# A hybrid decoder step on one Trainium2 core: the final rows with buffers of their own, and their residual sum on GpSimd

## What is computed

```python
    h = rmsnorm(x, norm2_g[l]) * (1 + sc2) + sh2
    x = x + g2 * moe(h, router_w, router_b, moe_w_gate[l], moe_w_up[l], moe_w_down[l])
y = rmsnorm(x, final_norm_g)
```

## Time and profile before

| | us |
|---|---|
| median of three runs | 1424.47 |
| the profiled execution, its own time | 1426.68 |
| its span in the profile | 1425.1 |
| busy in the span: PE, DVE, ACT, POOL | 1141.1, 699.1, 579.0, 127.0 |
| first gather of the final rows issued | 1362.7 |
| last normalisation ends | 1422.9 |
| POOL idle in the final stage because of stores | 25.8 |

### The profile page before, as it was taken

The page is one execution under the profiler, slowest core; times in us unless marked ns, Lnnn a source line. Parts: engine busy times, 40 slices in busy tenths (PEclk is TensorE's granted clock), DMA queues, the critical chain, the costliest instruction groups (busy, mean ns, idle before and its releaser), DMA issues.

```text
span 1425.1 us, 18556 instructions
## 1 busy us (share of the span) xinstructions
PE 1141.1 (80%) x6899; PEld 639.2 (45%) x6900; DVE 699.1 (49%) x1029; ACT 579.0 (41%) x850; POOL 127.0 (9%) x135
## 2 busy tenths in 40 slices
PE   3799579549898989898779995029899999999810
PEld 0355256436566666665444453014445544444400
DVE  2434334344435454544733335428765686656557
ACT  2222324133535353535531113027755566555433
POOL 0000001000000000000010000522111111111032
PEclk9899789759999999999798998559999999999955
DMA  9763200062313232383142440068977797779255
GB/s 344 282 227 142 54 0 0 9 167 55 100 49 90 60 90 60 90 295 103 47 121 68 140 163 31 0 236 321 381 267 261 290 373 276 284 257 368 103 189 182
DMA packets 122341, 234.43 MB, mean 164 GB/s; under 512 B 11079, under 2 KB 54569, under 8 KB 119200
## 3 DMA queue, kind: packets, MB, share of 16 engines
q1 hardware_dynamic: 111760, 200.37, 41.3%
q0 software_dynamic: 7200, 21.06, 4.0%
q10 hardware_dynamic: 3312, 12.06, 2.1%
HBM read 197.60 MB, written 35.64 MB: 164 GB/s over the span
## 4 chain that ended last, share of the span: by engine, by line
PE 63%; DVE 13%; DMA 10%; ACT 5%; issue 5%; POOL 2%; SPq 1%; DVEq 0%; POOLq 0%; ACTq 0%
PE banks L1576 7%; PE banks L1577 6%; PE banks L1578 6%; PE banks L1915 5%; PE banks L1917 5%; PE banks L1916 5%; PE banks L1737 3%; DMA arena<-in_moe_w_gate_dram 3%; PE banks L1751 2%; PE banks L1765 2%; DVE arena L1237 2%; PE banks L1934 2%; PE banks L1936 2%; PE banks L1935 2%; PE banks L1856 2%
## 5 line engine op out<-in xcount | busy, mean ns | idle before, releaser
L1469 DVE SCALAR_TENSOR_TENSOR arena<-arena 128x2048 f16<-128x2048 f32 x96 | 217.5, 2287 | 80.8 <-ACT arena L959 80.7
L959 ACT ACTIVATE arena<-arena 128x2048 f16<-128x2048 f32 x96 | 180.5, 1907 | 92.7 <-DMA arena<-in_moe_w_up_dram 53.8
L1576 PE MATMUL banks<-arena 128*128 128x384 f16 (+5 forms) x576 | 191.5, 332 | 16.1 <-DVE arena L1119 12.4
L1577 PE MATMUL banks<-arena 128*128 128x384 f16 (+5 forms) x576 | 190.9, 331 | 0.0
L1578 PE MATMUL banks<-arena 128*128 128x384 f16 (+5 forms) x576 | 190.7, 331 | 0.0
L1915 PE MATMUL banks<-arena 128*128 128x512 f16 x368 | 141.0, 383 | 9.8 <-DVE arena L1482 9.8
L1917 PE MATMUL banks<-arena 128*128 128x512 f16 x368 | 140.7, 382 | 0.0
L1916 PE MATMUL banks<-arena 128*128 128x512 f16 x368 | 140.6, 382 | 0.0
L854 ACT ACTIVATE arena<-banks 128x512 f32<-128x512 f32 (+3 forms) x96 | 49.3, 514 | 129.9 <-PE banks L1751 129.9
L1237 DVE CUSTOM_DVE_ANT_0 arena<-banks,arena 128x128 f32<-128x128 f32 (+7 forms) x96 | 72.3, 753 | 46.0 <-PE banks L1737 45.8
L846 ACT ACTIVATE arena<-arena 128x128 f32<-128x128 f32 (+7 forms) x96 | 74.3, 774 | 28.3 <-DVE arena L1240 27.2
(11 more groups left out here) (325 smaller groups left out, 1694.1 us busy)
## 6 DMA issues: line engine op xcount, KB each, us to landing
arena<-in_moe_w_gate_dram SPq DMA_DIRECT2D x32, 1024.0 KB, 8.6
arena<-in_moe_w_up_dram SPq DMA_DIRECT2D x32, 1024.0 KB, 8.3
arena<-in_moe_w_down_dram SPq DMA_DIRECT2D x32, 1024.0 KB, 6.5
arena<-in_w_ada_dram SPq DMA_DIRECT2D x24, 1024.0 KB, 7.5
slot_rows<-arena ACTq DMA_DIRECT2D x23, 512.0 KB, 6.8
out_dram<-arena SPq DMA_DIRECT2D x20, 512.0 KB, 2.6
arena<-in_w_in_dram SPq DMA_DIRECT2D x18, 512.0 KB, 7.0
arena<-in_x_prompt_dram SPq DMA_DIRECT2D x16, 512.0 KB, 8.6
```

Source lines behind the costliest of these rows:

```text
L959: A(w_hi[s][p // 2][:, (p % 2) * PIECE:(p % 2 + 1) * PIECE], stage[g % RING], ACT.Copy, scale=WS).then_inc(phi_ok, 1)
L1469: v.scalar_tensor_tensor(out=w_lo[s][p // 2][:, part], in0=stage[(PIECES * s + p) % RING], scalar=WS, in1=w_hi[s][p // 2][:, part], op0=AL ...
L1576: mm(out, hTh[:, k, tok], wh(k), start=(first and k == ks[0]), stop=False)
L1577: mm(out, hTh[:, k, tok], wl(k), start=False, stop=False)
```

## The change

Every tile gets a pair of buffers of its own: `yA` and `yB` have NT = 9 entries each instead of 4. The buffers lie where the experts' weights lay, which are no longer used. All stores count on a single semaphore, which SP waits for once at the end.

GpSimd issues the gathers of tiles 0 to 3. Then, in turn t of nine, it issues the gathers of tile t+4 if there is one, waits until VectorE has finished the gate product of tile t (new semaphore `gated_ok`), and does the residual sum of tile t itself. The wait for a store is gone. Before tile t's gathers it waits for `ya_in` of tile t-4, so that one semaphore counts only one pair of gathers at a time. VectorE's residual sum is taken out; the gate product no longer waits for its own completion and increments `gated_ok` instead. ScalarE's square waits for `res_ok` as before, which GpSimd now increments.

```diff
-        yA = [V(c0 + s * D, D) for s in range(YS)]
-        yB = [V(c0 + (YS + s) * D, D) for s in range(YS)]
-        sqj3 = V(c0 + 2 * YS * D, D)
-        assert c0 + 2 * YS * D + D <= A_X1
+        yA = [V(c0 + t * D, D) for t in range(NT)]
+        yB = [V(c0 + (NT + t) * D, D) for t in range(NT)]
+        sqj3 = V(c0 + 2 * NT * D, D)
+        assert c0 + 2 * NT * D + D <= A_X1
...
             for t in range(NT):
                 sp.wait_ge(norm_ok, 2 * NT + t + 1)
-                sp.dma_start(yp[t * P:(t + 1) * P] if t < PT else ys, yA[t % YS][0:rows_of(t)]).then_inc(y_out[t % YS], 16)
-            for s in range(YS):
-                sp.wait_ge(y_out[s], 16 * ((NT - s + YS - 1) // YS))
+                sp.dma_start(yp[t * P:(t + 1) * P] if t < PT else ys, yA[t][0:rows_of(t)]).then_inc(y_out, 16)
+            sp.wait_ge(y_out, 16 * NT)
...
+            def gather_rows(t):
+                n = rows_of(t)
+                if t >= YS:
+                    pool.wait_ge(ya_in[t % YS], 32 * (t // YS))
+                for j, dst in ((0, yA), (1, yB)):
+                    nc.gpsimd.indirect_dma_start(
+                        dst[t][0:n], None, slot_rows,
+                        bass.IndirectOffsetOnAxis(ap=ids[0:n, 2 * t + j:2 * t + j + 1], axis=0)).then_inc(ya_in[t % YS], 16)
+            for t in range(YS):
+                gather_rows(t)
             for t in range(NT):
                 n = rows_of(t)
-                if t >= YS:
-                    pool.wait_ge(y_out[t % YS], 16 * (t // YS))
-                for j, dst in ((0, yA), (1, yB)):
-                    nc.gpsimd.indirect_dma_start(
-                        dst[t % YS][0:n], None, slot_rows,
-                        bass.IndirectOffsetOnAxis(ap=ids[0:n, 2 * t + j:2 * t + j + 1], axis=0)).then_inc(ya_in[t % YS], 16)
+                if t + YS < NT:
+                    gather_rows(t + YS)
+                pool.wait_ge(gated_ok, t + 1)
+                nc.gpsimd.tensor_tensor(X1[0:n, t], X1[0:n, t], yA[t][0:n], ALU.add).then_inc(res_ok, 1)
...
                     lk.done(v.scalar_tensor_tensor(out=ya, in0=yb, scalar=w12[0:n, 2 * t + 1:2 * t + 2], in1=ya, op0=ALU.mult, op1=ALU.add))
-                    lk.done(v.tensor_tensor(ya, ya, g2b if t < PT else modrow(G2, NB), ALU.mult))
-                    v.tensor_tensor(X1[0:n, t], X1[0:n, t], ya, ALU.add).then_inc(res_ok, 1)
+                    v.tensor_tensor(ya, ya, g2b if t < PT else modrow(G2, NB), ALU.mult).then_inc(gated_ok, 1)
```

More of the change, by code:

```diff
@@ L398, in build @@
         phi_ok = sem("phi_ok"); plo_ok = sem("plo_ok")
-        ya_sc = sem("ya_sc")
+        ya_sc = sem("ya_sc"); gated_ok = sem("gated_ok")
         xgT_ps = sem("xgT_ps"); xgT_hi = sem("xgT_hi"); xgT_ok = sem("xgT_ok"); g_ps = sem("g_ps"); u_ps = sem("u_ps")
@@ L403, in build @@
         ya_in = [sem(f"ya_in{s}") for s in range(YS)]; mix_link = sem("mix_link"); rows_zero = sem("rows_zero")
-        y_out = [sem(f"y_out{s}") for s in range(YS)]
+        y_out = sem("y_out")
         stage_done = sem("stage_done")
@@ L1028, in _ @@
                     act.wait_ge(ya_in[t % YS], 32 * (t // YS + 1))
-                    ya = yA[t % YS][0:n]
+                    ya = yA[t][0:n]
                     A(ya, ya, ACT.Copy, scale=w12[0:n, 2 * t:2 * t + 1]).then_inc(ya_sc, 1)
@@ L1528, in _ @@
                     n = rows_of(t)
-                    ya, yb = yA[t % YS][0:n], yB[t % YS][0:n]
+                    ya, yb = yA[t][0:n], yB[t][0:n]
                     dve.wait_ge(ya_sc, t + 1)
@@ L1540, in _ @@
                 lk.done(v.reciprocal(rs[0:n, u:u + 1], rs[0:n, u:u + 1]))
-                v.scalar_tensor_tensor(out=yA[u % YS][0:n], in0=X1[0:n, u], scalar=rs[0:n, u:u + 1], in1=fng[0:n],
+                v.scalar_tensor_tensor(out=yA[u][0:n], in0=X1[0:n, u], scalar=rs[0:n, u:u + 1], in1=fng[0:n],
                                        op0=ALU.mult, op1=ALU.mult).then_inc(norm_ok, 1)
```

## The result

The changed kernel takes 1436.69 us, the median of seven runs (1433.1 to 1441.96), beside 1427.45 us for seven runs of the kernel before (1423.12 to 1430.51). The ratio is 1.0074 with a 95% interval of 1.005 to 1.0099, that is 7 to 14 us slower. I had forecast slower by 4.8 us, 1429.3, with a range up to 1433: the sign was right, the size about half of the 9.2 us between the medians. Of the distance from 1429.3 to 1436.69, 3.0 us are the kernel before itself, whose median is higher in seven runs than in the three I had.

The account below looks back on a forecast made before the run. VectorE nearly sets the pace, 45.41 of 52.40 us busy. Start to 1386.95, six tiles of 5.89 to 1422.3, tail 5.44: 1427.7 against 1422.90, +4.8, median 1429.3; own range 1427 to 1433, with faster rivals from 1417.

Parts of the forecast that it names:

- the start of the sum: Final rows, tiles 0 to 2: add 0 directly behind tile 1's gate product; tile 2's ends at 1386.95, 5.0 us lost.
- the sum: Last normalisation's end, added up from start, six tiles and tail: 1427.7 instead of 1422.90, +4.8 us.
- The length of the add: GpSimd's residual add per tile: 2.3 us, between two-pass ends of 2.08 (copy) and 2.60 (broadcast).
- Add and VectorE in one line: GpSimd's add and VectorE's three two-input instructions take turns per tile, swapping 1.22 us for 2.3 - 0.2.
- Tile time: Each of six tiles after tile 2: combine, gate product, wake, add's hold and normalisation, 5.89 us together.
- The tail: After tile 8's gate product: add, square, root, reciprocal and normalisation, 5.44 us.
- VectorE is not held: Rival: VectorE's normalisation and combine run beside the add, a clash costing only 0.2 us; -8 us, 1416.5; chance 0.15.
- GpSimd goes last: Rival: ready VectorE instructions pass the waiting add; tile 7.9 us, 12 us on top of the sum, 1441; chance 0.05.
- The shorter add: Rival: GpSimd's add takes 1.8 us, so about no change, or 1.04, so -6.5 us; chance 0.23.
- The gathers of tiles 5 to 8: Case: these gathers wait for adds instead of stores; tile 8 issued near 1395, needed near 1417, so hidden.

Follow-up runs that it names:

- the load moved away: Changed kernel plus one small GpSimd add of zeros far ahead, behind its last broadcast: 1428.8 us beside 1425.64 for the kernel before, ratio 1.0018.

## Why the prediction was wrong

- **The failed step** is the start of the sum: "Add 0 is behind it: 1376.05 to 1378.35". I priced the add by its duration and its place in the line, and put what GpSimd must do before a first add behind a broadcast at nothing, without a reason. Measured, add 0 started 8.35 us behind its gather. From the first combine to the end of tile 2's gate product the kernel before takes 11.4 us (1381.91 - 1370.55), the changed one 24.6 (1395.71 + 1.22 - 1372.31), and with the load moved away 16.0 (1383.38 + 1.22 - 1368.62): 4.6 lost there, where I had 5.0, and 8.6 more by the load.
- With that gap out of the way 4.75 is measured where the sum has 4.8. So near a hit is partly luck: the start costs 0.4 less than I had, and six tiles at 5.96 cost 0.4 more.
- It could have been seen. The trace of before has such configurations under the source line of the first broadcast, at 671.7 us, 58.6 ahead of that broadcast (730.3); the line stands below. There GpSimd waits 59.0 us for VectorE anyway, so a gap would not show, and I read past it. The Trainium skill, page "GPSIMD Engine Reference", section "Instruction dispatch", tells of about 6 us, 5.95 measured, for the first call to a freshly loaded kernel (there a piece of GpSimd's code), with no visible instruction. The traces here agree in that no instruction shows, but the gaps are longer, 6.95, 7.14, 8.06, 8.35 and 9.72 us, and the measurement decides.

```profile
L659 POOLq MODIFY_POOL_CONFIG  x2: 11/11/11, 671.7 to 671.7; - x2
```

- **The length of the add**, 2.3 by my choice between two passes of a copy and two of a broadcast: 2.34.
- **Add and VectorE in one line**: right for instructions with two SBUF inputs. A held normalisation ends 1.08 us behind the add's end (1402.97 + 2.34 = 1405.31, and 1406.39); with 1.28 of its own it was let go 0.20 before that end, the figure of the earlier trace rows. The "whole instruction" of the Trainium skill, page "SBUF — State Buffer", section "Who interferes with whom", is longer than these rows show; it stands there for VectorE's two-port modes, and of two SBUF inputs only that they contend. Tile time 5.96, forecast 5.89.
- **The tail**, gate product of tile 8 to the end of the last normalisation: 5.44 forecast, 1438.05 - 1432.64 = 5.41 measured.
- **The rivals.** "VectorE is not held" was wrong for this kernel and right in its price once the operands were moved. "GpSimd goes last" did not occur: no add of the changed kernel took over 2.35, and it was VectorE's normalisation that waited. The shorter add did not occur. The gathers of tiles 5 to 8 stayed hidden, as I had them: ScalarE waits for rows at the first two tiles only.
- Over whole runs the loss is 7 to 14 us; the stage's 13.4 lies inside, near the upper end.

## What to carry to other kernels

A kind of operation that GpSimd has not done just before can cost a gap that no instruction fills, here 7 to 10 us between broadcasts and adds. Look under its source line, and under those of its neighbours, for configurations that the program doesn't write, and place the first use where the engine waits anyway. Moving the sum from VectorE to GpSimd gained nothing while VectorE's instructions read two SBUF tiles, since the two then took turns and GpSimd's turn was the longer (2.34 against 1.22 us); with the second operand in accumulator banks they ran side by side. When a change has two parts, price them apart: here the buffers were worth 6 us, and the moved sum cost 11 by the adds that VectorE's work waits for, and 8.6 by the gap.

## What was not expected of the hardware

- Each change between a broadcast and an add on GpSimd costs a gap, 6.95 to 8.35 us ahead of the add and 9.72 ahead of the broadcast, with two pool configurations at its start. The copies and gathers between the early add at 836.62 and the next at 1373.70 have none and bring no gap back.
- An instruction that issues a gather stands in the line too: 1.76 us beside a VectorE instruction with two SBUF inputs, 0.94 in the mean when VectorE reads only one.
- VectorE takes 1.22 to 1.28 for 1024 columns whether its second input comes from SBUF or from the banks, and only the first kind is held.
